# Expert passes of 127 slots: stationary tiles of 127 columns in place of 128 in a two-layer trunk with a mixture of experts

## What is computed

```python
def moe_swiglu(h, w_router, w_gu, w_down):
    logits = (h @ w_router).astype(jnp.float32)
    top_v, top_i = lax.top_k(logits, TOP_K)
    gates = jax.nn.softmax(top_v, axis=-1)
    combine = jnp.sum(jax.nn.one_hot(top_i, N_EXPERTS) * gates[..., None], axis=-2)
    out = jnp.zeros_like(h)
    for e in range(N_EXPERTS):
        out = out + combine[..., e:e + 1] * swiglu(h, w_gu[e], w_down[e])
    return out
```

## Time and profile before

| | |
|---|---|
| median of three runs | 1547.66 us (1545.26 to 1547.7) |
| the profiled execution's own time | 1547.53 us |
| its span, first to last instruction | 1545.8 us |
| TensorE clock granted, mean | 0.991 of full |
| bytes moved by DMA | 476 MB, mean 308 GB/s |
| experts' first matmul, last matmul (start) | 583.75 us, 1532.6 us |

### The profile page before, as it was taken

How to read it: one execution, slowest core, us unless ns; L and a number is a source line. 1 busy time by engine, 2 the same in 40 slices (tenths; PEclk the granted TensorE clock), 3 DMA queues, 4 the chain that set the end, 5 groups by cost and what they waited for, 6 DMA issues and landing times.

```text
span 1545.8 us, 21011 instructions
## 1 busy us (share of the span) xinstructions
PE 1508.5 (98%) x7550; PEld 1263.7 (82%) x7550; DVE 1222.4 (79%) x1008; ACT 1020.5 (66%) x905; POOL 97.9 (6%) x115
## 2 busy tenths in 40 slices
PE   8899999999899999999999999999999999999997
PEld 7688888888889788788888888888888888888885
DVE  6665554456689858898898898898898998998996
ACT  5554444345688637777777777777777777777774
POOL 2042000000012214000000000000000000000020
PEclk9899999999999999999999999999999999999999
DMA  9369755545443438999999999999999999999997
GB/s 326 113 232 413 264 188 190 191 137 165 135 137 117 146 106 333 403 391 395 370 366 410 359 372 410 361 385 396 359 384 389 371 385 385 371 392 385 405 386 298
DMA packets 166229, 476.21 MB, mean 308 GB/s; under 512 B 9152, under 2 KB 35024, under 8 KB 166176
## 3 DMA queue, kind: packets, MB, share of 16 engines
q1 hardware_dynamic: 157152, 446.73, 77.7%
q0 software_dynamic: 5888, 19.23, 3.2%
q10 hardware_dynamic: 3136, 9.54, 1.5%
HBM read 454.49 MB, written 20.97 MB: 308 GB/s over the span
## 4 chain that ended last, share of the span: by engine, by line
PE 82%; issue 11%; DVE 2%; POOLq 1%; DMA 1%; ACT 1%; DVEq 1%; SPq 0%; POOL 0%; ACTq 0%
PE bank L781 26%; PE bank L783 26%; PE bank L782 26%; PE bank L1237 2%; DMA ring<-swa_w_qkv_in 1%; POOLq L395 1%; DVE w_lo L1354 1%; POOLq L393 0%; PE bank L1224 0%; PE bank L1001 0%; PE bank L806 0%; ACT w_hi L455 0%; PE bank L1292 0%; PE bank L1190 0%; PE bank L1213 0%
## 5 line engine op out<-in xcount | busy, mean ns | idle before, releaser
L1751 DVE TENSOR_TENSOR w_lo<-ring,w_hi 128x2048 fp32r<-128x2048 f32 x336 | 763.3, 2290 | 79.3 <-PE bank L783 73.1
L675 ACT ACTIVATE w_hi<-ring 128x2048 fp32r<-128x2048 f32 x336 | 635.7, 1919 | 141.3 <-DMA ring<-moe_w_gu_in 93.5
L781 PE MATMUL bank<-w_hi,xgT_hi 128*128 128x512 f32 x896 | 351.1, 392 | 3.4 <-DVE w_lo L1751 2.3
L783 PE MATMUL bank<-w_hi,xgT_lo 128*128 128x512 f32 x896 | 349.0, 390 | 0.0
L782 PE MATMUL bank<-w_lo,xgT_hi 128*128 128x512 f32 x896 | 348.6, 389 | 0.0
L1354 DVE TENSOR_TENSOR w_lo<-ring,w_hi 128x2048 fp32r<-128x2048 f32 (+1 forms) x84 | 194.9, 2323 | 116.0 <-ACT w_hi L455 115.2
L455 ACT ACTIVATE w_hi<-ring 128x2048 fp32r<-128x2048 f32 (+1 forms) x84 | 158.9, 1896 | 123.3 <-PE bank L783 116.6
L781 PEld LDWEIGHTS bank<-w_hi,xgT_hi 128*128 128x128 f32 x896 | 168.2, 188 | 38.0 <-DVE w_lo L1751 2.8
L783 PEld LDWEIGHTS bank<-w_hi,xgT_lo 128*128 128x128 f32 x896 | 168.2, 188 | 35.2
L782 PEld LDWEIGHTS bank<-w_lo,xgT_hi 128*128 128x128 f32 x896 | 168.3, 188 | 34.2
L781 PE MATMUL bank<-w_hi,m_hT_hi 128*128 128x512 f32 x448 | 175.8, 392 | 0.0
(11 more groups left out here) (337 smaller groups left out, 1634.4 us busy)
## 6 DMA issues: line engine op xcount, KB each, us to landing
ring<-moe_w_gu_in SPq DMA_DIRECT2D x230, 1024.0 KB, 7.0
ring<-moe_w_down_in SPq DMA_DIRECT2D x112, 1024.0 KB, 7.1
ring<-ffn_w_gu_in SPq DMA_DIRECT2D x28, 1024.0 KB, 6.7
ring<-ffn_w_down_in SPq DMA_DIRECT2D x14, 1024.0 KB, 4.8
xg_rows<-zeros POOLq DMA_DIRECT2D x36, 256.0 KB, 12.6
ring<-ssm_w_in_in SPq DMA_DIRECT2D x8, 1024.0 KB, 5.1
ring<-ssm_w_in_in SPq DMA_DIRECT2D x16, 512.0 KB, 3.9
ring<-ssm_w_in_in SPq DMA_DIRECT2D x32, 256.0 KB, 4.4
```

What stands on the lines that cost most here:

```text
L675: act.activation(w_hi[:, c % HI], ring[:, c % RING], ACT.Copy).then_inc(hi_ready, 1)
L781: pe.matmul(o, stat[0], mov[0], start=start, stop=False)
L783: return pe.matmul(o, stat[1], mov[0], start=False, stop=stop)
L1751: dve.tensor_tensor(w_lo[:, c % SPLIT], ring[:, c % RING], w_hi[:, c % HI].bitcast(F32), ALU.subtract).then_inc(lo_ready, 1)
```

## The change

A pass holds 127 slots (CAP) in place of 128. The tiles in memory keep 128 rows. In the experts, every stationary tile of gate, up and down is cut to its first 127 columns, the matmuls' outputs to 127 partitions, and Silu, multiply and the transposes of `m_hh` to 127 rows. Slots of places 127 to 253 go to the second pass and those of 254 and up to a third, which the arrays and the bounds of `last_i` now allow for: `xg_rows` has 26 tiles, `y_rows` 24, and 43 tiles are cleared by 86 DMAs. The slot arithmetic between the counts and `slots_i` has more steps. Layer 0, the Mamba block, the making of expert 0's tile and the transposes of the other experts' rows keep 128.

```diff
 E = 8
+CAP = 127
+PASSES = -(-T // CAP)
 
...
         last_i = sb("last_i", [P, 1], I32)
-        xg_rows = nc.dram_tensor("xg_rows", (2 * E + 2, P, D), F32).ap()
-        y_rows = nc.dram_tensor("y_rows", (2 * E, P, D), F32).ap()
+        xg_rows = nc.dram_tensor("xg_rows", (PASSES * E + 2, P, D), F32).ap()
+        y_rows = nc.dram_tensor("y_rows", (PASSES * E, P, D), F32).ap()
 
...
             return sm[:, t, q].rearrange("p (a x i) -> p x a i", a=2, x=2)[:, part]
+
+        CLEARED = 16 * 2 * ((PASSES * E + 2) + (PASSES * E - (E - 1)))
 
...
                         allow_small_or_imprecise_dtypes=True).then_inc(column_ready, 1)
-            for i in range(2 * E + 2):
+            for i in range(PASSES * E + 2):
                 for a in range(2):
...
 
-            for i in range(E - 1, 2 * E):
+            for i in range(E - 1, PASSES * E):
                 for a in range(2):
                     pool_e.dma_start(y_rows[i][:, 512 * a:512 * (a + 1)], zeros[:]).then_inc(rows_cleared, 16)
-            pool_e.wait_ge(rows_cleared, 2 * (3 * E + 3) * 16)
+            pool_e.wait_ge(rows_cleared, CLEARED)
             pool_e.wait_ge(c_pad, 1)
...
                             act.wait_ge(m_h, it * NJ + (2 * j - 2 + i + 1))
-                        act.activation(m_sg[:, i], bank[i][:], ACT.Silu).then_inc(m_silu, 1)
+                        act.activation(m_sg[0:CAP, i], bank[i][0:CAP], ACT.Silu).then_inc(m_silu, 1)
                     ahead_e(it, up + LEAD, up + LEAD + 1)
...
             pe.wait_ge(r_passes, 1)
-            last = pe.value_load(last_i[0:1, 0:1], min_val=E - 1, max_val=2 * E - 1)
+            last = pe.value_load(last_i[0:1, 0:1], min_val=E - 1, max_val=PASSES * E - 1)
 
...
                     for a in range(4):
-                        ins = pe.transpose(bank[4 + f % 2][:, a * P:(a + 1) * P], m_hh[:, f % 2, a * P:(a + 1) * P],
-                                           ident[:])
+                        ins = pe.transpose(bank[4 + f % 2][:, a * P:a * P + CAP], m_hh[0:CAP, f % 2, a * P:(a + 1) * P],
+                                           ident[0:CAP, 0:CAP])
                     ins.then_inc(m_T, 1)
...
                                 for k in range(k_tiles):
-                                    ins = product(bank[2 * gu + i][:], part((xgT_hi, xgT_lo), k_tiles * q + k),
+                                    ins = product(bank[2 * gu + i][0:CAP], part((xgT_hi, xgT_lo), k_tiles * q + k, slice(0, CAP)),
                                                   part(wv, k, slice(512 * i, 512 * (i + 1))), q == 0 and k == 0,
...
                         for i in range(2):
-                            ins = product(bank[6 + i][:], part((m_hT_hi, m_hT_lo), 2 * c + k),
+                            ins = product(bank[6 + i][0:CAP], part((m_hT_hi, m_hT_lo), 2 * c + k, slice(0, CAP)),
                                           part(wv, k, slice(512 * i, 512 * (i + 1))), c == 0 and k == 0,
...
                 dve.tensor_scalar(after, tri_lt[:], -float(2 ** 100), None, ALU.mult)
-                dve.wait_ge(rows_cleared, 2 * (3 * E + 3) * 16)
+                dve.wait_ge(rows_cleared, CLEARED)
                 dve.tensor_scalar(decay_of, left, bot, top, ALU.mult, ALU.add)
...
             dve.tensor_reduce(rt[:, 9, 0:1], bank[0][:, 0:E], AXX, ALU.max)
-            dve.tensor_scalar(r3[6], place, P - 0.5, float((E - 1) * P), ALU.is_gt, ALU.mult)
-            dve.drain()
-            dve.tensor_scalar(rt[:, 9, 1:2], rt[:, 9, 0:1], P + 0.5, float(E), ALU.is_gt, ALU.mult)
+            dve.tensor_scalar(r3[6], place, CAP - 0.5, float(E * P - CAP), ALU.is_gt, ALU.mult)
+            dve.tensor_scalar(r3[15], place, 2 * CAP - 0.5, float(E * P - CAP), ALU.is_gt, ALU.mult)
+            dve.drain()
+            for i in range(1, PASSES):
+                dve.tensor_scalar(rt[:, 9, 2 + i:3 + i], rt[:, 9, 0:1], i * CAP + 0.5, float(E), ALU.is_gt, ALU.mult)
             dve.tensor_tensor(r3[6], r3[6], first_slot[:], ALU.add)
             dve.drain()
-            dve.tensor_scalar(last_i[:], rt[:, 9, 1:2], float(E - 1), None, ALU.add).then_inc(r_passes, 1)
+            dve.scalar_tensor_tensor(last_i[:], rt[:, 9, 3:4], float(E - 1), rt[:, 9, 4:5], ALU.add,
+                                     ALU.add).then_inc(r_passes, 1)
+            dve.tensor_tensor(rt[:, 9, 1:2], rt[:, 9, 3:4], rt[:, 9, 4:5], ALU.add)
+            dve.tensor_tensor(r3[6], r3[6], r3[15], ALU.add)
+            dve.drain()
             dve.tensor_tensor(r3[6], r3[6], place, ALU.add)
...
                             dve.wait_ge(m_T, it * NJ + (f - 1))
-                        dve.tensor_tensor(m_hh[:, i], m_sg[:, i], bank[2 + i][:], ALU.mult).then_inc(m_h, 1)
+                        dve.tensor_tensor(m_hh[0:CAP, i], m_sg[0:CAP, i], bank[2 + i][0:CAP], ALU.mult).then_inc(m_h, 1)
 
```

More of the change, by code:

```diff
@@ L327, in _ @@
             sp.wait_ge(r_passes, 1)
-            last = sp.value_load(last_i[0:1, 0:1], min_val=E - 1, max_val=2 * E - 1)
+            last = sp.value_load(last_i[0:1, 0:1], min_val=E - 1, max_val=PASSES * E - 1)
             with sp.Fori(0, last, E) as first:
@@ L403, in _ @@
             pool_e.wait_ge(r_passes, 1)
-            last = pool_e.value_load(last_i[0:1, 0:1], min_val=E - 1, max_val=2 * E - 1)
+            last = pool_e.value_load(last_i[0:1, 0:1], min_val=E - 1, max_val=PASSES * E - 1)
             pool_e.sem_inc(y_free, 1)
@@ L700, in _ @@
             act.wait_ge(r_passes, 1)
-            last = act.value_load(last_i[0:1, 0:1], min_val=E - 1, max_val=2 * E - 1)
+            last = act.value_load(last_i[0:1, 0:1], min_val=E - 1, max_val=PASSES * E - 1)
             def rows_split(it):
@@ L1834, in _ @@
             dve.wait_ge(r_passes, 1)
-            last = dve.value_load(last_i[0:1, 0:1], min_val=E - 1, max_val=2 * E - 1)
+            last = dve.value_load(last_i[0:1, 0:1], min_val=E - 1, max_val=PASSES * E - 1)
             def shares():
```

## The result

The changed kernel takes 1570.22 us, the median of 4 runs (1568.96 to 1571.5), beside 1547.47 us for the kernel before in 4 runs of the same comparison: a ratio of 1.0148, with a 95% interval of 1.0135 to 1.016. It is **22.8 us slower**, where 39.5 us of gain were forecast; 1570 lies outside the range of 1501 to 1549. The profiled execution took 1568.96 us with a span of 1566.8, which is 21.0 more than before.

A forecast was written before the change was run, and what follows sets the result against it. TensorE, 98% busy with float32r matmuls, was taken as the bound. 1547.5 - 42.7 + 1.9 + 1.1 + 0.2 gave 1508 us; range 1501 to 1549, the forecast's own 1501 to 1516.

The forecast's parts named there:

- Step 1: In the experts' 4032 matmuls, 127-column stationary tiles save 10.6 ns each, for a pace of 216.0 ns: -42.7 us.
- Slower: Rival, chance 0.17: expert tiles of 127 columns are fetched through the moving path, +39.6 ns a matmul, 1708 us.
- No change: Rival, chance 0.12: the 13.3 ns per expert matmul belong to float32r, not to tile width; 1548 us.
- The DMA feed caps it: Rival, chance 0.09: only 393 GB/s lasts through the experts, so an expert takes 114.7 us; 1520 us.
- Step 2: First expert: the ring's refill data come no sooner, so TensorE gives back its gain before the stall, +1.9 us.
- Step 3: After the first expert's stall: VectorE and DMA (399 GB/s) cover TensorE only thinly, +1.1 us, between 0 and 8.
- Steps 4 and 5: Four more small VectorE operations in the slot arithmetic, +0.2 us; 32 more zero-fill DMAs beside busy TensorE, 0.
- Step 6: Experts' Silu, multiply and transposes on 127 rows: their time goes with columns, which stay, so 0.

The follow-up runs named there:

- bf16 kernel: The kernel before with the experts' two-part operands held in bf16 in place of float32r, 128 columns kept: 1507.34 us, ratio 0.9735.

## Why the prediction was wrong

**Step 1 failed**, and with it the sum: "That looks like a pause in what feeds the array: a load of a full tile, in four strips side by side". The rows showed a remainder of 13.3 ns with float32r at 2.4 GHz and none with fp32 or at half the clock, and all rows of it had 128 columns. Two causes fitted, the type and the width. I took the width, because 13.3 ns is the time of 32 columns and a rule gave the same 32. That agreement was chance: with 512 moving columns the remainder is 13.3 to 20 ns for every float32r width from 2 to 128 columns, and 2.5 for bf16 with 96, 127 or 128. Instead of -10.6 ns, the 127-column tile from column 0 cost +6.67 ns. No row of before could show that, since the float32r tiles in those rows are all full.

One row spoke against it and was left to a rival: loads of float32r and of fp32 "both last about 0.19 us". Had the float32r load been in four strips, it should have been shorter than fp32's; in bf16, where the short load exists, it shows as 98 ns beside 138. The trace of the kernel before also had the answer outright, in the source of each load: one run of 128 columns, no strips.

**The rivals.** *Slower* had the side right. Its mechanism is refuted: the forecast of 266.3 ns, a fetch of 127 columns through the moving path, would go with the number of columns, while 96 columns lose less than 127 and 127 from column 1 lose nothing. *No change* had the right owner of the 13.3 ns and missed the new 6.67. *The DMA feed caps it* was wrong where it could be tried: the bf16 kernel draws 398 GB/s through the experts.

**Step 2** (+1.9 us given back by the first expert) could not show in the changed kernel. It shows in the bf16 kernel, which has the pace that it assumed, and it was too small: the first expert gives back about 4.2 us there. 1.4 of them are longer waiting for `w_lo_e` and most of the rest is the lower clock after the wait, which the step didn't reckon with. **Step 3** (+1.1, an expert in 113.0 us at 399 GB/s) held in the middle experts, where an expert takes 112.71 us at 398 GB/s without a wait. In the last expert TensorE waits 1.3 us, and about 2 us of its gain are lost.

That the bf16 kernel came to 1507.34 us beside the 1508 of the sum is thus in part luck. In its trace a middle expert saves 5.65 us, eight times which is 45 where the sum has 42.7, and the first and the last give back some 6 where it has 3.0; the experts also begin 0.8 us later. The sum was right in kind about what follows from a pace of 216 ns, and wrong that 127 columns give it.

**Steps 4 and 5** (+0.2 and 0) held within what can be measured: with the full columns the change measures 1.0002. The fills lie wholly under TensorE's work. **Step 6** held: the transposes on 127 rows take 1.02 us from the last matmul before to the first after, as those on 128 rows do.

**The range** reached to "no change" as its slow end. Step 1 said itself that such tiles are not in the trace, but between a loss of nothing and the +39.6 ns of the rival it named no smaller loss. No row pointed at one of some ns, and no row excluded it.

**What stays open**: why a float32r matmul takes 13.3 ns over its streaming, why the end of the stationary tile in memory adds 6.7, why other counts of moving columns change or turn round its effect, whether bf16 tiles that start elsewhere than at column 0 have any, and why the same code in the last expert, and in 58 matmuls of one other execution, ran at the other pace. None of the kernels separates these causes.

## What to carry to other kernels

When a remainder is found in only one shape and one type, both are suspects; a quiet series of 36 matmuls over widths, places and types takes 270 us of one program and would have settled it. With 512 moving columns, keep float32r stationary tiles whole, or cut them at the front so that they still end where the whole tile did: here a cut at the end cost 3% of every matmul, and one at the front nothing. For other moving counts measure both, since with 496 the cut tile was the faster. If the numbers allow two bf16 parts, the type is where the 11 ns a matmul are. A faster TensorE then waits longer where the feed is late, and a wait of 3.6 us cost it the full clock for a dozen matmuls besides.

## What was not expected of the hardware

- With 512 moving columns, where a stationary tile lies in its row changes the pace: the same 127 columns of float32r take 233.3 ns from column 0 and 227.3 from column 1; 128 columns take 227.7, 233.3 and 226.7 from columns 0, 3 and 64. In bf16 128, 127 and 96 columns from column 0 do not differ (215.8).
- float32r has the plain load at every width (189 ns at 128 columns, fp32 190); only bf16 shows a short one, 98 ns at 128 columns.
- The effect of the cut depends on the moving columns, and its sign too: 128 and 127 columns from column 0 take 173.3 and 176.8 ns for 384 of them, 119.8 both for 256, and 223.3 and 220.2 for 496.
- The same float32r matmuls on tiles of the same place can run at either pace: 233 ns in seven down products of the changed kernel and 227 in the eighth.
- In the bf16 kernel matmuls ran at the 1.2 GHz level, 427 ns apart, for twelve steps after a wait of 3.6 us. After the wait of 2.3 us in the kernel before they did not.
